# One transformer kernel, three edits: late queries spread over ninety rows of the expert stage, rotations of the latent attention from doubled weight columns, and an earlier slot return with the last side gate by halves

## The reference

```python
u = rmsnorm(x, g_mix) @ w_in            # recurrent branch, latent attention, branch gates
q = (rmsnorm(cq) @ w_qup)               # 8 heads of 64 + 32 columns; the 32 are rotated by position
q_rope = apply_rope_2(q[..., 64:], cos, sin); k_rope = apply_rope_2(kr, cos, sin)
x = x + merged @ w_out                  # the two branches, gated
# experts: per token and head, two lists of 128 key scores, top 16 of each, top 16 of the sums
s = einsum(q_half, sub_keys); eidx, gate = top16(...), softmax(...)
x = x + sum(gate * gelu(expert_u[eidx] . h) * expert_v[eidx])     # 8 heads x 16 experts
x = x + (p @ w_ple_proj) * sigmoid(rmsnorm(x, g_ple) @ w_ple_gate)
return rmsnorm(x, g_final)
```

## Time and profile before

| what | value |
|---|---|
| median of 3 runs | 2235.29 us (2230.26 to 2239.66) |
| profiled execution, its own time | 2243.22 us |
| its span, first to last instruction | 2241.4 us |
| PE busy / DVE / ACT / POOL | 91% / 56% / 42% / 16% |
| bytes read from HBM | 486.74 MB |
| mean granted clock of PE | 0.970 |

### The profile page before, as it was taken

The page is one execution under the profiler, slowest core; times in us unless marked ns, Lnnn a source line. Parts: engine busy times, 40 slices in busy tenths (PEclk is TensorE's granted clock), DMA queues, the critical chain, the costliest instruction groups (busy, mean ns, idle before and its releaser), DMA issues.

```text
span 2241.4 us, 35977 instructions
## 1 busy us (share of the span) xinstructions
PE 2034.2 (91%) x14354; PEld 1649.6 (74%) x14354; DVE 1264.2 (56%) x2327; ACT 948.4 (42%) x1857; POOL 362.8 (16%) x415
## 2 busy tenths in 40 slices
PE   7999989999999999999988999977888887788887
PEld 7999979999999988999877888764444333334434
DVE  5554645655655564655655444344566667767654
ACT  5444445444443554544555232223333444543543
POOL 0000010000000100000000232012344434443350
PEclk9999999999999999999999999999999999899898
DMA  9553506563655421755304110357999999999994
GB/s 314 189 186 123 182 17 226 175 200 132 206 182 175 151 96 52 247 190 170 115 20 145 45 40 21 118 217 279 371 395 411 383 385 411 408 414 382 391 418 158
DMA packets 218019, 489.64 MB, mean 218 GB/s; under 512 B 9840, under 2 KB 170128, under 8 KB 184992
## 3 DMA queue, kind: packets, MB, share of 16 engines
q0 software_dynamic: 37024, 268.52, 29.6%
q1 hardware_dynamic: 177104, 214.32, 29.5%
q10 hardware_dynamic: 3760, 5.02, 0.7%
HBM read 486.74 MB, written 1.05 MB: 218 GB/s over the span
## 4 chain that ended last, share of the span: by engine, by line
PE 75%; DMA 8%; DVE 8%; ACT 6%; issue 3%; POOL 0%; DVEq 0%; POOLq 0%; ACTq 0%
PE bank L795 74%; DMA arena_sb<-peer_uv,arena_sb 7%; DMA con_sb<-peer_uv,arena_sb 1%; DVE sq_sb L2823 1%; ACT arena_sb L2163 1%; ACT arena_sb L2159 1%; DVE arena_sb L2702 1%; DVE arena_sb L2699 1%; ACT L2126 0%; DVE arena_sb L2734 0%; DVE arena_sb L2731 0%; DVE arena_sb L2737 0%; DVE parts_sb L2223 0%; ACT L2130 0%; PE bank L986 0%
## 5 line engine op out<-in xcount | busy, mean ns | idle before, releaser
L795 PE MATMUL bank<-arena_sb 64*64 64x64 f32 (+9 forms) x3944 | 627.0, 339 | 124.4 <-ACT arena_sb L2163 107.7
L795 PEld LDWEIGHTS bank<-arena_sb 64*64 64x64 f32 (+4 forms) x3944 | 343.3, 162 | 392.4 <-issue 202.1
L795 PE MATMUL bank<-xh_sb,parts_sb 128*128 128x256 f32 x3328 | 604.2, 284 | 19.7 <-DVE parts_sb L2218 16.4
L795 PEld LDWEIGHTS bank<-xh_sb,parts_sb 128*128 128x128 f32 x3328 | 513.8, 189 | 26.1 <-issue 25.1
L795 PE MATMUL bank<-xl_sb,parts_sb 128*128 128x256 f32 x1808 | 509.3, 282 | 0.0
L2218 DVE TENSOR_TENSOR parts_sb<-ring_sb,parts_sb 128x2048 fp32r<-128x2048 f32 x132 | 298.7, 2290 | 173.1 <-ACT parts_sb L1684 173.1
L795 PEld LDWEIGHTS bank<-xl_sb,parts_sb 128*128 128x128 f32 x1808 | 343.1, 190 | 0.0
L2930 POOL DMA_INDIRECT arena_sb<-peer_uv,arena_sb x220 | 246.1, 1118 | 448.6 <-PE bank L795 353.3
L1684 ACT ACTIVATE parts_sb<-ring_sb 128x2048 fp32r<-128x2048 f32 x132 | 248.0, 1910 | 69.8 <-PE bank L795 68.5
L795 PE MATMUL bank<-h_high_sb,parts_sb 128*128 128x256 f32 x1408 | 255.8, 282 | 0.0
L795 PEld LDWEIGHTS bank<-h_high_sb,parts_sb 128*128 128x128 f32 x1408 | 218.1, 190 | 0.0
(11 more groups left out here) (290 smaller groups left out, 1938.8 us busy)
## 6 DMA issues: line engine op xcount, KB each, us to landing
ring_sb<-ffn_w_gate SPq DMA_DIRECT2D x44, 1024.0 KB, 5.4
ring_sb<-ffn_w_up SPq DMA_DIRECT2D x44, 1024.0 KB, 6.8
ring_sb<-ffn_w_down SPq DMA_DIRECT2D x44, 1024.0 KB, 5.0
ring_sb<-w_in SPq DMA_DIRECT2D x17, 1024.0 KB, 6.0
ring_sb<-w_in_ab SPq DMA_DIRECT2D x12, 1024.0 KB, 5.2
ring_sb<-w_out SPq DMA_DIRECT2D x12, 1024.0 KB, 5.3
ring_sb<-w_in_cd SPq DMA_DIRECT2D x12, 1024.0 KB, 5.4
ring_sb<-peer_w_q SPq DMA_DIRECT2D x8, 1024.0 KB, 5.8
```

The source lines that it names most:

```text
L795: return pe.matmul(dst, lhsT, rhs, start=start, stop=stop_, skip_group_check=loose)
```

## The change

The late work of the experts is indexed by the row, not by (u, e), and is spread over rows 4 to 99; `scores` is a step of its own, and ACT evicts each step after the diagonal of the next row. The norm of block 1 goes ahead of row 0, with head 2's eviction behind its squares, and ACT's chances of unit 0 ahead of both. `best_keys` moves from e = 5 to 7 and `best_sums` from 9 to 11. The host lays the 32 rotated columns of the query and key weights out twice, the second time with halves swapped (`turned`), so that the product gives both; `turns()` is gone, one `angle` of 64 rows gives sine and cosine, and three operations rotate all queries. `soft_scores` returns the owed slot in the latent attention. The last side gate is worked off by halves, and the final norm's weight is applied ahead of its root.

```diff
-        LATE = {(u, e): ("query", 3 + u, BOTH, c) for u in range(1, 5) for e, c in ((7, 0), (15, 1))}
-        LATE[5, 15], LATE[6, 15] = ("ple", 0, 0, 0), ("ple", 4, 0, 0)
-        for j in range(2 * EARLY_HEADS):
-            LATE[0, 2 + j + (j > 4)] = ("query", j // 2, 1, j % 2)
-        LATE[0, 0], LATE[0, 9] = ("norm", 1, 0, 0), ("tokens", 1, 0, 0)
-        LATE[0, 11], LATE[0, 13] = ("query", EARLY_HEADS, BOTH, 0), ("query", EARLY_HEADS, BOTH, 1)
+        LATE = {}
+        for r, h in ((4, 0), (7, 1), (10, 2)):
+            LATE[r], LATE[r + 1], LATE[r + 2] = ("query", h, 1, 0), ("query", h, 1, 1), ("scores", h, 1, 0)
+        LATE[13] = ("tokens", 1, 0, 0)
+        for r, h in ((15, 3), (26, 4), (42, 5), (58, 6), (74, 7)):
+            LATE[r], LATE[r + 3], LATE[r + 4] = ("query", h, BOTH, 0), ("query", h, BOTH, 1), ("scores", h, BOTH, 0)
+        LATE[90], LATE[96] = ("ple", 0, 0, 0), ("ple", 4, 0, 0)
...
-            for j in range(5):
-                plan(("mrot", j), 4 + j % 2)
...
-            fetch(at["rope"], slot(at["rope"], KC, 32), rows(w2)[:, :, 2304:2336])
+            fetch(at["rope"], slot(at["rope"], KC, 64), rows(A["w_rope_2"]))
...
-            fetch(k, slot(k, 2, 768), rows(A["mla_w_qup_2"][0]))
+            fetch(k, slot(k, 2, 1024), rows(A["w_qup_2"]))
...
                         ins = mm(b[e][:, a : a + w], q_of(l, h)[:, qb * P : (qb + 1) * P], k_of(l, h)[:, 0:w], True, not ext)
+                        if l == 2 and qb == 0:
+                            release(ins)
...
-                chunks(4)
-                turns()
-                for i in range(5, 8):
+                for i in range(4, 8):
                     chunks(i)
...
                 tokens(0)
                 out_block(1)
                 queries(2, 0)
+                norm_block(1)
                 for u in range(16):
...
-                act.wait_ge(S("angle_ready"), 2)
-                act.activation(SINM[64:96, :], ANG[64:96, :], ACT.Sin).then_inc(S("trig_ready"), 1)
-                act.activation(COSM[64:96, :], ANG2[64:96, :], ACT.Sin).then_inc(S("trig_ready"), 1)
+                act.wait_ge(S("angle_ready"), 1)
+                act.activation(TRIG[64:128, :], ANG[64:128, :], ACT.Sin).then_inc(S("trig_ready"), 1)
...
-                queries_out(2, 0)
...
+                chances(0)
+                act.preload_act_table_set("natural_log_exp_and_others")
                 squares7(1)
-                chances(0)
+                queries_out(2, 0)
+                root7(1)
+                act.preload_act_table(ACT.Gelu)
...
-                        if (u, e) in LATE:
-                            kind, first, part, c = LATE[u, e]
+                        if n - 1 in LATE:
+                            kind, first, part, c = LATE[n - 1]
...
-                for j in range(4):
-                    b = take(dve, ("mrot", j))
-                    give(dve.tensor_tensor(TMPM[r, 2 * j : 2 * j + 2, :], b[r, 0:512].rearrange("p (a b) -> p a b", a=2), sin2, ALU.mult),
-                         ("mrot", j))
-                link(dve.tensor_tensor(QM[r, :, :], QM[r, :, :], COSM[r, :].unsqueeze(1).broadcast_to([32, 8, T]), ALU.mult))
...
+                link(dve.tensor_tensor(TMPM[cos_of, :, :], QM[sin_of, :, :], eight(sin_of), ALU.mult))
+                link(dve.tensor_tensor(QM[cos_of, :, :], QM[cos_of, :, :], eight(cos_of), ALU.mult))
+                dve.tensor_tensor(QM[cos_of, :, :], QM[cos_of, :, :], TMPM[cos_of, :, :], ALU.add).then_inc(S("mrope_ready"), 1)
...
+                        dve.wait_ge(S("last_gate"), i + 1)
+                        link(dve.tensor_tensor(GATE[:, QUAD[i], :], GATE[:, QUAD[i], :], PLE[:, QUAD[i], tokens_of(tb)], ALU.mult))
+                        xs = xT[:, QUAD[i], tokens_of(tb)]
+                        dve.tensor_tensor(xs, xs, GATE[:, QUAD[i], :], ALU.add).then_inc(S("tail_x"), 1)
...
+                    dve.wait_ge(S("tail_rstd"), tail_step(9, tb) + 1)
+                    for i in range(2):
+                        dve.tensor_tensor(xn[:, QUAD[i], tokens_of(tb)], XG[:, QUAD[i], :],
+                                          rstd[:, tokens_of(tb)].unsqueeze(1).broadcast_to([P, 4, P]), ALU.mult).then_inc(S("tail_xn"), 4)
...
-                residual_block(1)
                 chances(0)
+                residual_block(1)
...
                         if n == 2:
                             norm_block(1)
...
-                            if e == 5:
+                            if e == 7:
...
-                            if e == 9:
+                            if e == 11:
...
-                side(1)
-                normed(9, 1)
...
+    turned = lambda w: np.concatenate([w, w[..., 16:32], w[..., 0:16]], -1)
```

More of the change, by code:

```diff
@@ L57 @@
     ("ones", 128), ("eps", 4), ("ident", 128), ("heads", 128), ("suffix", 128), ("after", 128), ("causal", 384),
-    ("dilated", 384), ("cos", 256), ("sin", 256), ("turn", 128), ("turn_mla", 32), ("seen", 512),
-    ("level", 2 * 6 * 64), ("eye", 64), ("inv", 1), ("count", 16), ("one", 1),
+    ("dilated", 384), ("cos", 256), ("sin", 256), ("turn", 128), ("seen", 512),
+    ("level", 2 * 6 * 64), ("eye", 64), ("inv", 1), ("quarter", 2), ("count", 16), ("one", 1),
 ):
@@ L101, in constants @@
     put("turn", turn)
-    turn = np.zeros((P, 32))
-    for j in range(16):
-        turn[64 + 16 + j, j] = -1.0
-        turn[64 + j, 16 + j] = 1.0
-    put("turn_mla", turn)
     put("seen", np.concatenate([row < col, row <= col, row > col, row >= col], 1))
@@ L119, in constants @@
     v = np.zeros((P, 1))
-    v[64:96, 0] = np.tile(inv2, 2)
+    v[64:128, 0] = np.concatenate([inv2, inv2, -inv2, inv2])
     put("inv", v)
+    v = np.zeros((P, 2))
+    v[64:96, 0], v[64:96, 1] = 0.25, 0.5 * np.pi
+    put("quarter", v)
     put("eps", np.tile(np.array([[EPS, GN_EPS, 1e-24, 0.0]]), (P, 1)))
@@ L1162, in rope_key @@
                     have(at["rope"])
-                    w = slot(at["rope"], KC, 32)
+                    w = slot(at["rope"], KC, 64)
                     b = fill_begin(pe, ("u", 18))
@@ L1231, in queries_keys @@
                 kq = at["mla"]
-                wq, wkv = slot(kq, 2, 768), slot(kq + 1, 1, 1024)
+                wq, wkv = slot(kq, 2, 1024), slot(kq + 1, 1, 1024)
                 have(kq)
@@ L1246, in queries_keys @@
                     fill_end(mm(b[0:64, 0:T], wkv[:, 0, h * P : h * P + 64], CKVN, True, True), ("mk", h))
-            def turns():
-                for j in range(5):
-                    b = fill_begin(pe, ("mrot", j))
-                    if j < 4:
-                        emptied(pe, ("mq", 2 * j))
-                        emptied(pe, ("mq", 2 * j + 1))
-                        src = QM[64:96, 2 * j : 2 * j + 2, :].rearrange("p a b -> p (a b)")
-                    else:
-                        emptied(pe, ("u", 18))
-                        src = KR[64:96, :]
-                    for n0 in range(0, 512 if j < 4 else T, T):
-                        ins = mm(b[64:96, n0 : n0 + T], C("turn_mla", 32)[64:96, :], src[:, n0 : n0 + T], True, True)
-                        if j + n0 == 0:
-                            release(ins)
-                    fill_end(ins, ("mrot", j))
             def lora():
@@ L1520, in query @@
                         owed[0] += part > 0
-                        scores(h, part)
                 def queries(h, part):
@@ L1525, in queries @@
                         query(h, part, c)
+                    scores(h, part)
                 def tokens(tb):
@@ L1562, in weighted_rows @@
                         ins.then_inc(S("row_used"), 1)
-                        if (u, e) in LATE:
-                            kind, m, part, c = LATE[u, e]
+                        if n in LATE:
+                            kind, m, part, c = LATE[n]
                             if kind == "query":
                                 query(m, part, c)
-                            elif kind == "norm":
-                                norm_block(m)
+                            elif kind == "scores":
+                                scores(m, part)
                             elif kind == "tokens":
@@ L1888, in second_in @@
                 b = take(act, ("u", 18))
-                give(act.activation(KR[64:96, :], b[64:96, 0:T], ACT.Copy), ("u", 18))
+                give(act.activation(KR[64:128, :], b[64:128, 0:T], ACT.Copy), ("u", 18))
                 def chunks(i):
@@ L2059, in query_out, with scores_out @@
                     give(act.activation(QP[:, qp_of(h, part, c), cols], b[:, cols], ACT.Copy), ("pq", h, part, c))
-                    if c == 0:
-                        return
+                def scores_out(h, part):
                     b = take(act, ("sc", h, part))
@@ L2070, in queries_out @@
                         query_out(h, part, c)
+                    scores_out(h, part)
                 def tokens_out(tb):
@@ L2163, in experts @@
```

(10 more changed lines are left out.)

63 lines of the change are left out of this document (31 added, 32 removed).

## The result

The changed kernel takes 2213.20 us (median of 17 runs, 2208.05 to 2229.93), the kernel before 2239.58 us over 17 runs of its own (2226.63 to 2245.03). The ratio is 0.9896, with a 95% interval of 0.9879 to 0.9912. The change wins 26 us between the medians (23 us by the ratio), where I had forecast 51, and 2213 lies above my range. The direction was right and the size was half.

A forecast was written before the change was run, and what follows sets the result against it. PE bounds the kernel up to about 1430 us, the gathers' DMA (about 421 GB/s) in the experts. Gains 27 + 8 + 0 + 9 + 6 + 1 = 51 us off the 2235.3 median give 2184; range 2172 to 2197.

The forecast's parts named there:

- I expect 27 of the 29 us: Start of experts, to row 25: spreading the queries keeps the gather queue full, winning 27 us of idle DMA time; bounds 16 to 29.
- Rivals 1 and 2: Start of experts: PE-ACT handshake partly stays, about 2203, chance 0.19; or spreading does nothing, 2219, chance 0.06.
- Of the 12.5 us idle I expect 8 back: Experts, units 1 to 4: spreading late queries and scores over four rows wins 8 us; bounds 3 and 11.
- it fits with 1.5 us to spare: Experts: after the moved top 16, row 13's buffer is freed 1.5 us before the queue would suffer, costing nothing.
- Top 16 moved ... I take zero: Experts: moving the top 16 two rows costs nothing; bounds for units 6 to 15 are 5 lost, 4 gained.
- Rival 3: Experts: top 16 against table loads empties the queue in each of 13 units; 65 us lost, 2249, chance 0.08.
- a gap above 8 us: Experts: the forecast expected no POOL issue gap above 8 us in units 1 to 4; gaps around row 13 would contradict it.
- In all 58 us: Experts: total idle DMA time before the change, 29 us to row 25, 12.5 to row 105, 16.5 to row 255.
- some 25 us larger: Experts: by the skill's estimated 2.41 us per queued row, idle time and possible gain would be some 25 us larger.
- Rotations 9: Second block's entry: without `turns()`, DVE's low half of the eighth chunk comes earlier, winning 9 us; bounds 6 and 11.
- Slot return 6: Start of the recurrence: early slot return removes the 5.32 us weight wait and some slow clock, 6 us; bounds 4 and 8.
- Tail 1: Kernel's end: eight operations become two wide ones and side work goes under PE, winning 1 us; bounds 0 and 2.

The follow-up runs named there:

- the best kernel: Changed kernel with late queries of heads 4 to 7 six rows earlier, ACT's chances behind e = 3, and 30 unused constant columns: 2197.70 us, 0.9817 of before.
- The shift by hand: Kernel before with 32 unused constant columns (128 bytes per partition) behind the others, nothing else changed: 2251.09 us, 1.0055 of before.
- the padding: 30 unused constant columns restoring old addresses: on before with rotations alone 2231.82 us; on the changed kernel 2211.44 us, again 2209.63 us.
- its unpadded twin: Changed kernel with late queries of heads 4 to 7 six rows earlier and ACT's chances behind e = 3, without unused columns: 2209.59 us, 0.9844 of before.

## Why the prediction was wrong, point by point

**"I expect 27 of the 29 us" at the start: right.** The queue stays full. The first issue and the dot of row 25, which I wanted 85 to 90 us later, in the changed kernel:

```profile
1468.86 1.05 POOL L2913 DMA_INDIRECT arena_sb<-peer_uv,arena_sb  x1 [83.32 <-DVE arena_sb L2720]
...
1554.18 1.23 DVE L2808 CUSTOM_DVE_ANT_0 sq_sb<-arena_sb,con_sb 128x1024 f32<-128x1024 f32 x1 [0.66 <-DMA arena_sb<-peer_uv,arena_sb]
```

85.3 us. The window behind 1488 reads 408 GB/s where the earlier trace rows had 284. In idle time 24.6 us went; in time to row 25 it is 30.6, as 2.5 MB of weights, 6 us, were left for later. I had counted eight slots of weights into that stretch in both kernels, and the full queue of gathers pushes some of them out of it. Rivals 1 and 2 are out.

**"Of the 12.5 us idle I expect 8 back" in units 1 to 4: the step that failed first.** The idle time stayed at 12 to 13 us. My reason was that spread steps leave no long stretch without a row, and the stretches did shrink: POOL's longest wait for a buffer is 5.30 us, where the earlier trace rows had 9.46. But it is their sum that drains a queue of seven buffers. One unit of the changed kernel, over all engines:

```profile
1663.67 1.28 ACT L2106 ACT_TABLE_LOAD   x1
...
1663.70 3.62 PE L790 MATMUL bank<-arena_sb 128*128 128x512 f32 x4 [2.61 <-ACT arena_sb L2147]
...
1664.96 0.31 ACT L2108 ACTIVATE arena_sb<-arena_sb 128x16 f32<-128x16 f32 x1
...
1667.60 1.31 POOL L2913 DMA_INDIRECT arena_sb<-peer_uv,arena_sb  x1 [5.30 <-PE bank L790]
...
1669.51 3.62 PE L790 MATMUL bank<-xn_sb,ring_sb 128*128 128x256 f32 x16
...
1675.12 1.16 POOL L2913 DMA_INDIRECT con_sb<-peer_uv,arena_sb  x1 [3.79 <-PE bank L790]
...
1677.89 1.23 DVE L2808 CUSTOM_DVE_ANT_0 sq_sb<-arena_sb,con_sb 128x1024 f32<-128x1024 f32 x1 [2.41 <-DMA arena_sb<-peer_uv,arena_sb]
...
1683.91 1.23 DVE L2808 CUSTOM_DVE_ANT_0 sq_sb<-con_sb 128x1024 f32<-128x1024 f32 x1 [4.79 <-DMA con_sb<-peer_uv,arena_sb]
```

`best_sums` ends at about 1661. PE, having waited 2.61 us, does two rows at half its clock, which takes as long as ACT's two table loads, then two more; then the second half query of e = 13 takes 3.62 us, and the scores follow behind e = 14. Five issues of POOL from 1656.5 to 1675.1 stand 4.7 us apart on average, where 2.49 would keep the queue as it is, and some 10 us later the dots wait 2.41 and 4.79 us for data instead of 1.26. I had checked the top 16 against the seven buffers (it fits with 1.5 us to spare) and the late queries against them (3.6 us at most), each by itself, and never laid the one behind the other, though the new table puts them there. Four runs show that it is the coincidence: moving the queries away, or moving the table loads away, leaves about 6 us idle of 12.9, and both together 5.7 and, padded, 4.7. Each breaks up the same heap, which is why they do not add. The longest wait for a buffer is not what counts: it is 5.84 us with the queries moved and 7.48 in the best kernel, both longer than after's 5.30. Nor were there 12.5 us to win, but some 7. In the four windows with 4.7 to 6.1 us left the DMA share is 1.01 at 409 to 412 GB/s: by that share the engines were full, and what is left comes of counting with 421 GB/s, the rate of gathers alone.

**"Top 16 moved ... I take zero": the sum of two errors.** In units 1 to 4 the move is worth 236.2 - 225.8 = 10.5 us by the windows and 26.4 - 12.9 = 13.5 us by idle time, since behind e = 9 the top 16 meets both half queries. So the spreading alone costs these units what the move gives back, and the two make 0 where I had 8 and 0. In the units without late queries it costs a little. Rows 105 to 255 take 391.4 us with the top 16 in its old place and 392.7 in the new, but over all traces there is a pattern: 392.7 to 396.7 us in the five kernels with the top 16 late and the table loads behind e = 12, 388.2 to 391.4 in the four where one of the two was moved away. That is some 4 us between the means, within my bound of 5 lost. It is not proven, as the kernel before and its variants range from 390.0 to 394.2. Rival 3 named the place rightly (the queue runs dry behind the top 16) but for all 13 units and as a loss against before; it is mostly four units, and a gain not made. My sign for it, a gap above 8 us, would have missed it.

The Trainium skill ("ScalarE: Activation LUTs", What ACT_TABLE_LOAD costs) has a drain of about 1.38 us beside each load. The rows above do not show one: the load of 1.28 us starts 0.02 us behind the operation before it and ends at 1664.95, and the Exp starts at 1664.96.

**"In all 58 us" behind row 105.** I left the late units at 16.5 us idle, and they have 20.5 by the windows (17.6 before). The executions of this study range there from 388.2 to 396.7 us, so 3 us of one pair say little; the pattern above says more. (The "some 25 us larger" of the prediction is 267 transfers at 0.08 us, so some 22.)

**The first block, which no step of mine touched: +10.9 us.** I went by the diff's operations and had nothing for the constant `turn_mla` leaving. It takes 128 bytes out of every partition, and all that lies behind moves. The shift by hand costs the kernel before the same 10 us in the first block and 12 in all (10 between the medians); the padding takes them back with the rotations alone (11.5 us), and in the best kernel against its unpadded twin (12 us between the medians, part of which is the low clock of two of the twin's four executions). In the changed kernel the first block becomes 8 us shorter by it, but the whole by only 2 us between the medians (its two sets of runs stand at 0.9884 and 0.9863 of before, against 0.9896, which is 3 and 7 us). The entry stage takes 1.4 us back in both padded traces and in the best kernel's (86.3 us at a granted clock of 0.96, against 84.9 at 0.98). What takes the rest, if anything does, stays open, and so does how the address acts on PE.

**Rotations 9: right.** DVE in the changed kernel:

```profile
1150.10 2.29 DVE L2219 TENSOR_TENSOR parts_sb<-ring_sb,parts_sb 128x2048 fp32r<-128x2048 f32 x1 [15.79 <-ACT parts_sb L1678]
...
1157.06 2.28 DVE L2486 TENSOR_TENSOR arena_sb<-arena_sb 32x2048 f32<-32x2048 f32 x1
1159.38 2.29 DVE L2219 TENSOR_TENSOR parts_sb<-ring_sb,parts_sb 128x2048 fp32r<-128x2048 f32 x1
```

The low half of the eighth chunk starts 1159.38 - 1101.40 = 58.0 us behind the stage's first product, against 68.3 in the earlier trace rows; no 32x32 product is left. With the rotations alone and the arena in place it is 59.2 us, 9.1 less than before, so the step that I had forecast is right in both. The whole stage is 9.3 us shorter here, part of it by a granted clock of 0.98 in place of 0.93, and 6.8 us there.

**Slot return 6: 3.1 or 4.8, by execution.** The stage is 48.98 us in this trace. Over all traces with the early return it is 49.0 six times and 50.7 three times (the return alone, and two variants of the changed kernel, all three at a granted clock of 0.97, as was one of the six); without the return it is 53.6 to 54.4. What decides between the two is not shown. The wait for `w_in` is gone and the gate products start at once:

```profile
1208.97 7.07 PE L790 MATMUL bank<-xn_sb,ring_sb 128*128 128x256 f32 x32
1218.40 14.05 PE L790 MATMUL bank<-xn_sb,ring_sb 128*128 128x256 f32 x64 [2.36 <-ACT arena_sb L1942]
```

Behind the second of them PE now waits 2.36 us until ACT has emptied the bank: I had written that what follows "is ready", and it was ready only behind 5 us of delay.

**Tail 1: about 0.5.** The 2.3 us of the profiled pair are mostly the clock: at granted clocks of 0.84 and 0.85 the old tail takes 34.2 to 34.5 us and the new one 33.8 to 33.9; at 0.90 it is 32.5 to 32.6 and 32.1. That is within its bounds.

**The sum.** In the experts, 8 us forecast for units 1 to 4 became a loss of 6.6 (14.6 in all, 6 of them bytes that moved there from the start), the start gave 3.6 more, and the rest lost 2.7: 13.7 us are missing. The first block misses 10.9, the slot 1.2, and rotations and tail gave 1.6 more than forecast. That is 24.2 of the 24.6 us missing; the recurrence's 8.7 us and the luck of the profiled executions (8.8 us) nearly cancel. The match is closer than single traces deserve, since the entry and the tail hold some 2 us of clock each. The median of before moved as well: from 2235.3 us over three runs to 2239.6 over 17, which would have put the forecast at 2189, still too low.

## What to carry to other kernels

When a queue hides stalls, lay all stalls of a period on one line before crediting a cover: two that fit one at a time do not fit in a row, and what drains it is the sum of delays over as many rows as it has buffers, not the longest gap. When an edit removes or resizes a constant or buffer, ask what is allocated behind it, and measure the edit with the old addresses kept by padding before judging it. And take the difference of two profiled executions stage by stage with the granted clock beside each: a stage that nobody touched shows at once what belongs to the execution.

## What the runs showed of the hardware

- **A shift of 128 bytes costs 0.9% of a stage bound by PE.** The same 8408 matmuls are busy 1054.0 to 1057.4 us with the arena at its old address (seven traces) and 1064.2 to 1065.5 us with it 128 bytes off, in either direction (six), all at a granted clock of 1.00; a seventh shifted one took 1079.5 us at 0.98. From 600 to 1080 us it is 3808 or 3809 matmuls against 3775 to 3777.
- **A full queue of gathers starves the other loads.** 1 MiB of query weights took a median of 27.3 us to land, one load of the projection 51.1, against 5.8 where the gathers left gaps. Where both share the engines they move 408 to 412 GB/s, gathers alone 421.
- **A short wait can cost PE its clock.** Behind 2.61 and 5.30 us of waiting, two rows of products took 3.62 and 3.78 us, at granted clocks of 0.54 and 0.50, in place of 1.98: the 1.2 GHz level in place of 2.4. Not every wait does: behind 1.88 us two rows took 1.98. Per execution the mean granted clock of the changed kernel ran from 0.962 to 0.979; the two executions at 0.962 and 0.965 took 2229.8 and 2229.9 us, the others 2208.1 to 2219.1.
